# Seven half-size block products for the value tiles of a feed-forward layer, and an earlier value evacuation in latent attention

## The reference, cut to what matters

```python
q = (_rmsnorm(cq, q_norm) @ w_uq).reshape(B, S, H, MLA_QK)
kv = (_rmsnorm(ckv, kv_norm) @ w_ukv).reshape(B, S, H, MLA_NOPE + MLA_V)
k_nope, v = kv[..., :MLA_NOPE], kv[..., MLA_NOPE:]
```

```python
h = _rmsnorm(x, norm_g)
up = h @ w_up
gate, val = up[..., :D_FF], up[..., D_FF:]
gate = conv(gate, conv_w) + conv_b          # width 3 along the tokens
return (jax.nn.silu(gate) * val) @ w_down   # D_FF = 2816
```

## Time and profile before

| | us |
|---|---|
| median of 3 runs | 2328.27 (2326.47 to 2335.23) |
| the profiled execution | 2325.44 |
| its span, first to last instruction | 2323.6 |
| latent attention up to its loop of scores | about 194 to 235 |
| up projection of `ffn0` | 359 to 577 |
| first tile of its down projection | 577 to 592 |

### The profile page before, as it was taken

How to read it: one execution, slowest core, us unless ns; L and a number is a source line. 1 busy time by engine, 2 the same in 40 slices (tenths; PEclk the granted TensorE clock), 3 DMA queues, 4 the chain that set the end, 5 groups by cost and what they waited for, 6 DMA issues and landing times.

```text
span 2323.6 us, 30116 instructions
## 1 busy us (share of the span) xinstructions
PE 2245.7 (97%) x11716; PEld 1073.1 (46%) x11716; DVE 1298.2 (56%) x2620; ACT 1249.5 (54%) x2233; POOL 241.7 (10%) x324
## 2 busy tenths in 40 slices
PE   7999999999999999999999998999999999999998
PEld 3434554444444454444444446654334444654333
DVE  5565856456546556777664594654335744644233
ACT  7544666657657676665675763732225765522213
POOL 0000000000002330000000000021242000011232
PEclk9999999999999999999999999999999999999999
DMA  5230021331223211222123321468974231358997
GB/s 204 90 111 1 1 73 73 109 109 71 105 107 113 78 73 37 92 109 108 63 100 111 109 78 46 158 244 355 416 296 185 109 145 41 134 181 325 418 407 272
DMA packets 70576, 340.36 MB, mean 146 GB/s; under 512 B 13237, under 2 KB 13547, under 8 KB 55565
## 3 DMA queue, kind: packets, MB, share of 16 engines
q1 hardware_dynamic: 49680, 261.38, 29.4%
q0 software_dynamic: 20752, 77.04, 9.3%
HBM read 367.93 MB, written 28.34 MB: 171 GB/s over the span
## 4 chain that ended last, share of the span: by engine, by line
PE 86%; DVE 6%; ACT 3%; DMA 2%; issue 2%; POOL 1%; DVEq 0%; SPq 0%; POOLq 0%; ACTq 0%
PE PB L406 12%; PE PB L401 12%; PE PB L407 12%; PE PB L3417 8%; PE PB L3443 4%; PE PB L1753 3%; PE PB L1757 3%; PE PB L1754 3%; PE PB L470 1%; PE PB L471 1%; PE PB L472 1%; PE PB L3366 1%; DVE WS L321 1%; DMA T<-moe_x,small 1%; PE PB L4068 1%
## 5 line engine op out<-in xcount | busy, mean ns | idle before, releaser
L406 PE MATMUL PB<-AS,WS 128*128 128x512 f16 x1336 | 507.2, 380 | 4.8 <-DVE WS L321 4.8
L407 PE MATMUL PB<-AS,WS 128*128 128x512 f16 x1336 | 507.1, 380 | 0.0
L401 PE MATMUL PB<-AS,WS 128*128 128x512 f16 x1336 | 479.4, 379 | 2.5 <-DVE AS L1221 2.5
L321 DVE SCALAR_TENSOR_TENSOR WS<-raw,sc,WS 128x1024 f16<-128x1024 f32 (+3 forms) x288 | 329.2, 1191 | 89.5 <-ACT WS L308 89.5
L308 ACT ACTIVATE WS<-raw,sc 128x1024 f16<-128x1024 f32 (+3 forms) x288 | 288.5, 1057 | 77.0 <-DVE sc L288 74.9
L262 ACT ACTIVATE junk<-raw 128x1024 f16<-128x1024 f32 (+3 forms) x288 | 280.0, 972 | 7.0
L3417 PE MATMUL PB<-T 128*64 128x512 f32 x736 | 212.4, 595 | 11.9 <-issue 9.1
L406 PEld LDWEIGHTS PB<-AS,WS 128*128 128x128 f16 x1336 | 130.9, 98 | 165.4 <-DVE WS L321 5.5
L401 PEld LDWEIGHTS PB<-AS,WS 128*128 128x128 f16 x1336 | 130.8, 98 | 161.5 <-DVE AS L1221 4.1
L407 PEld LDWEIGHTS PB<-AS,WS 128*128 128x128 f16 x1336 | 130.9, 98 | 158.3 <-issue 4.8
L276 POOL PARTITION_ALL_REDUCE sc<-sc x72 | 31.6, 439 | 1250.9 <-ACT junk L262 1239.1
(11 more groups left out here) (667 smaller groups left out, 3653.0 us busy)
## 6 DMA issues: line engine op xcount, KB each, us to landing
T<-in_moe_up SPq DMA_DIRECT2D x26, 2048.0 KB, 12.7
raw<-in_w_up SPq DMA_DIRECT2D x22, 2048.0 KB, 7.7
T<-in_moe_down SPq DMA_DIRECT2D x26, 1024.0 KB, 14.5
raw<-in_w_down SPq DMA_DIRECT2D x16, 1408.0 KB, 6.0
raw<-in_w_in_even SPq DMA_DIRECT2D x8, 2048.0 KB, 7.8
raw<-in_w_in_odd SPq DMA_DIRECT2D x8, 2048.0 KB, 7.6
WS<-in_moe_up SPq DMA_DIRECT2D x6, 2048.0 KB, 16.2
moe_y<-X SPq DMA_DIRECT2D x18, 512.0 KB, 11.1
```

Source lines behind the costliest of these rows:

```text
L321: e.scalar_tensor_tensor(lo[q], raw[q], s, hi[q], MUL, SUB).then_inc(*k.s("dve_split").up("lo", i, q))
L401: return e.matmul(bank, wh[:, q, c, :], act.lo[c], start=False, stop=c == kt - 1)
L406: e.matmul(bank, wh[:, q, c, :], act.hi[c], start=c == 0, stop=False)
L407: e.matmul(bank, wl[:, q, c, :], act.hi[c], start=False, stop=False)
```

## The change

**In the up projection of `ffn0`**, chunks 3 to 10 (`SEVEN_FROM = 3`) keep their two gate tiles. Their two value tiles are a product of a 256 x 1024 by a 1024 x 512 matrix. It is cut into 2 x 2 blocks on the weight side (two output tiles by two halves of the inputs) and 2 x 2 on the activation side (two halves of the inputs by two halves of the tokens). It is then computed as seven block products instead of eight. Each product is 12 matmuls of 128 x 256 (4 input blocks, 3 parts). Three products use weight blocks as they are, four use sums of blocks, and so it is on the activation side.

- The activation sums are made once, during t = 5 to 9: four DVE sums, four ACT high parts, four DVE low parts, each of 128 x 1024.
- The weight sums are made for each chunk by POOL in fp32 (`pool_seven`: one operation of 128 x 1024 and two of 128 x 512), split by ACT and DVE (`act_seven_hi`, `dve_seven_lo`: parts "1" of 1024, "t" of 2048 and "b" of 512 elements). This happens in the chunk's own time, no longer in that of the chunk before. Only the two gate quarters are still split a chunk ahead.
- The products are put together by one ACT operation (`act_seven`) and five DVE operations (`dve_seven`), and two DVE products with the gate follow. They run behind the chunk, in the next one's time.
- The sum over partitions for the chunk's scale moves from POOL to PE: a matmul with ones of 4 columns behind the gate tiles. It waits for the four squares of the next chunk. So do the two sums for the scales of `hid`; the first stands in chunk 8, the second in the first down tile.
- The high and low parts of hidden tiles 0 to 15 are made in chunks 8, 9 and 10 by the table `SEVEN_EARLY`, at the end of each chunk's list.
- The down projection now waits, before its first matmul, for the last assembly (`up` of chunk 10), since the products lie in banks 4 to 7.
- The normed activation is kept in fp32 in `k.h`, as the sums need it.

**In latent attention**, PE makes queries 3 before it turns queries 0; ACT evacuates values 0 and turned queries 1 before the root for queries 3 and values 1 before the table load; DVE handles queries 2 before turned queries 0.

```diff
@@ even0_pe
     turned("k", 2)
+    queries(3)
     turned("q", 0)
-    queries(3)
     turned("k", 3)
@@ even0_act, query_squares
+        if j == 3:
+            values(0)
+            turned("q", 1, 0)
         w.wait_ge(*v.past("qss", j))
         act_root(e, m.qss[:, 8 * j:8 * j + 8], 96, k.col("eps6"), a, "q", j)
         if j == 3:
+            values(1)
             e.preload_act_table_set(LN_EXP)
@@ even0_dve
-    queries(0)
-    queries(1)
+    for j in range(3):
+        queries(j)
     turned(0)
-    queries(2)
     turned(1)
@@ new
+def pool_seven(k, e, w, n):
...
+    w.wait_ge(*k.s(f"raw{n % 2}").past(n))
+    if is_seven(n - 1):
+        w.wait_ge(*k.s("dve_split").past("lo", n - 1, "t"))
...
+    e.tensor_tensor(t[:, 0:1024].rearrange("p (a b) -> p a b", a=2), raw[:, 3072:4096].rearrange("p (a b) -> p a b", a=2),
+                    by2[:, :, 1024:1536], SUB).then_inc(*g.up("t13", n))
+    w.wait_ge(*g.now())
+    e.tensor_tensor(t[:, 1024:1536], raw[:, 3584:4096], t[:, 0:512], SUB).then_inc(*g.up("t2", n))
+    w.wait_ge(*g.now())
+    e.tensor_tensor(t[:, 1536:2048], raw[:, 1536:2048], t[:, 1024:1536], SUB).then_inc(*g.up("t", n))
@@ new
+def pe_seven(k, e, w, i, act):
...
+    for q in (0, 2):
+        t = 4 * i + q
+        w.wait_ge(*v.past("conv", t // 2 - 2))
+        pe_tile(k, e, w, name, t, act, k.PB[q][:, :], False)
+    w.wait_ge(*k.s("act_junk").past("w", n + 1, 3))
...
+    e.matmul(z.weight, k.cst("ones"), st, start=True, stop=True).then_inc(*p.up("sum", n + 1))
+    if i == EARLY // 2:
+        w.wait_ge(*v.past("sum", "hid", 0))
+        e.matmul(z.total, k.cst("ones"), k.small[:, 288:289], start=True, stop=True).then_inc(*p.up("total", "hid", 0))
...
+        for c in range(4):
+            e.matmul(out, w_hi[c], a_hi[c], start=c == 0, stop=False, skip_group_check=True)
+            e.matmul(out, w_lo[c], a_hi[c], start=False, stop=False, skip_group_check=True)
+            x = e.matmul(out, w_hi[c], a_lo[c], start=False, stop=c == 3, skip_group_check=True)
...
+    product(z.P1, ..., "P1", 1)
+    product(z.P6, ..., "P6", "t")
+    product(z.P2, ..., "P2")
+    product(z.P7, ..., "P7")
+    product(z.P5, ..., "P5")
+    product(z.P4, ..., "P4")
+    product(z.P3, ..., "P3", "b")
@@ new
+def dve_seven(k, e, w, i):
...
+    e.scalar_tensor_tensor(u2, z.P6, sc, p1, MUL, ADD)
+    e.scalar_tensor_tensor(z.up[:, 0, :], z.P2, sc, p1, MUL, ADD)
+    e.scalar_tensor_tensor(u34, two(z.P75), sc, u2.unsqueeze(1).to_broadcast([128, 2, 256]), MUL, ADD)
+    e.scalar_tensor_tensor(z.up[:, 3, :], z.P5, sc, u34[:, 0, :], MUL, ADD)
+    e.scalar_tensor_tensor(z.up[:, 1:3, :], two(z.P43), sc, u34, MUL, ADD)
@@ new
+SEVEN_EARLY = {8: range(0, 4), 9: range(4, 10), 10: range(10, 16)}
@@ ffn_pe
+    if not layer:
+        for i in range(SEVEN_FROM, UPS):
+            pe_seven(k, e, w, i, act)
+
     def free(bank):
+        if not layer:
+            w.wait_ge(*v.past("up", UPS - 1))
@@ ffn_act
+            for part in (1, "t", "b"):
+                act_seven_hi(k, e, w, n, part)
+            act_square(k, e, w, n + 1, 0)
+            act_square(k, e, w, n + 1, 1)
+            act_evac(k, e, w, m.up, 4 * i)
+            conv(2 * i, k.PB[0][:, :])
+            act_square(k, e, w, n + 1, 2)
+            act_square(k, e, w, n + 1, 3)
+            gate(2 * i)
+            if i > SEVEN_FROM:
+                square(2 * i - 2)
+                square(2 * i - 1)
+            act_evac(k, e, w, m.up, 4 * i + 2)
+            conv(2 * i + 1, k.PB[2][:, :])
+            hi_quarter(n + 1, 0)
+            gate(2 * i + 1)
+            hi_quarter(n + 1, 2)
+            act_seven(k, e, w, i)
...
+            for x in SEVEN_EARLY.get(i, ()):
+                hi(x)
@@ ffn_dve
+            if i > SEVEN_FROM:
+                hids(i - 1)
+            for part in (1, "t", "b"):
+                dve_seven_lo(k, e, w, n, part)
+            k.s("dve_split").mark("lo", n, 3)
+            taps(i)
+            conv(2 * i, k.PB[0])
+            if i == EARLY // 2:
+                total(0)
+            dve_seven_scale(k, e, w, n + 1)
+            if i == EARLY // 2:
+                scale(0)
+            conv(2 * i + 1, k.PB[2])
+            for q in ((0, 2) if is_seven(n + 1) else range(4)):
+                dve_lo_quarter(k, e, w, n + 1, q)
+            for x in SEVEN_EARLY.get(i, ()):
+                lo(x)
+        hids(UPS - 1)
+        total(1)
```

More of the change, by code:

```diff
@@ L505, in act_square_sum, with norm_tile @@
     e.activation(k.junk[:, 0:S], a, ACT.Square, accum_out=k.small[:, 256 + i:257 + i]).then_inc(*k.s("act_junk").up(*event))
+def norm_tile(k, stage, tmp, i):
+    return k.h[i] if stage == "ffn0" else tmp[i % 2]
 def dve_norm(k, e, w, stage, name, tmp):
@@ L539, in act_norm @@
         w.wait_ge(*v.past("h", "norm", i))
-        e.activation(k.as_hi[i], tmp[i % 2], ACT.Identity, scale=k.sc[:, 64 + which:65 + which]).then_inc(
+        e.activation(k.as_hi[i], norm_tile(k, stage, tmp, i), ACT.Identity, scale=k.sc[:, 64 + which:65 + which]).then_inc(
             *a.up("hi", "norm", i))
@@ L1159, in even0_act @@
     query_squares(3)
-    values(0)
-    turned("q", 1, 0)
-    values(1)
     values(2)
@@ L1704, in ffn_pool @@
         s5_pool(k, e, w)
+    if layer == 0:
+        pool_ahead(k, e, w, m.up, range(4 * SEVEN_FROM))
+        for i in range(SEVEN_FROM, UPS):
+            pool_seven(k, e, w, FIRST[m.up] + i)
+        pool_sum(k, e, w, place(m.down, 1)[0])
+        pool_ahead(k, e, w, m.down, range(1, 8))
+        return
     for g, tiles in enumerate((range(2 * EARLY), range(2 * EARLY, 2 * FF))):
@@ L1718, in ffn_pe @@
     act = k.normed_parts(m.stage, 2 * layer + 1)
-    for t in range(2 * FF):
+    for t in range(2 * FF if layer else 4 * SEVEN_FROM):
         if t >= 4:
@@ L1750, in pe_down @@
             w.wait_ge(*act.hi_ready(c))
+        if c == EARLY // 2 and (name, t) == ("w_down0", 0):
+            w.wait_ge(*act.sig.past("sum", "hid", 1))
+            e.matmul(seven_at(k).total, k.cst("ones"), k.small[:, 288:289], start=True, stop=True).then_inc(
+                *k.s("pe_ffn0").up("total", "hid", 1))
         if c == EARLY:
@@ L1786, in gate, with conv, square, hi_quarter @@
         e.activation(m.cv[i % 3], m.cv[i % 3], ACT.Silu).then_inc(*a.up("gate", i))
-    for t in range(2 * FF):
+    def conv(i, bank):
+        w.wait_ge(*v.past("taps", i // 2))
+        if i >= 3:
+            w.wait_ge(*v.past("hid", i - 3))
+        e.activation(m.cv[i % 3], bank, ACT.Identity, scale=m.tap[(i // 2) % 2][:, 1, i % 2:i % 2 + 1],
+                     bias=k.col(f"cb{layer}", i)).then_inc(*a.up("conv", i))
+    def square(i):
+        w.wait_ge(*v.past("hid", i))
+        act_square_sum(k, e, w, i, m.hid[i], m.stage, "hid", i)
+    def hi_quarter(n, q):
+        if not is_seven(n) or q % 2 == 0:
+            act_hi_quarter(k, e, w, n, q)
+    for t in range(2 * FF if layer else 4 * SEVEN_FROM):
         i = t // 2
@@ L1853, in scale @@
     def scale(g):
-        w.wait_ge(*k.s(f"pool_{m.stage}").past("total", "hid", g))
+        if layer == 0:
+            w.wait_ge(*k.s("pe_ffn0").past("total", "hid", g))
+            e.tensor_copy(k.small[:, 289:290], seven_at(k).total).then_inc(*v.up("total", "hid", g))
+            w.wait_ge(*v.now())
+        else:
+            w.wait_ge(*k.s(f"pool_{m.stage}").past("total", "hid", g))
         scale_of(e, w, v, k.small[:, 289:290], 20, m.s[g], m.inv[g], k.small[:, 290:291], "inv", "hid", g)
@@ L1859, in lo, with lo_quarter, taps, conv @@
         e.scalar_tensor_tensor(m.lo[i], m.hid[i], m.s[int(i >= EARLY)], m.hi[i], MUL, SUB).then_inc(*v.up("lo", "hid", i))
-    for t in range(2 * FF):
+    def lo_quarter(n, q):
+        if not is_seven(n) or q % 2 == 0:
+            dve_lo_quarter(k, e, w, n, q)
+    def taps(i):
+        n = FIRST[m.up] + i
+        dve_tile_scale(k, e, w, m.up, 4 * i, act)
+        src = k.cols[:, COL[f"cw{layer}"][0]:COL[f"cw{layer}"][0] + 3 * FF].rearrange("p (j t) -> p j t", j=3)
+        w.wait_ge(*k.s("dve_split").past("sc", n))
+        e.tensor_scalar(m.tap[i % 2], src[:, :, 2 * i:2 * i + 2], k.tile_scale(n), None, MUL).then_inc(*v.up("taps", i))
+    def conv(i, b):
+        c, tap = m.cv[i % 3], m.tap[(i // 2) % 2]
+        w.wait_ge(*v.past("taps", i // 2))
+        w.wait_ge(*a.past("conv", i))
+        e.scalar_tensor_tensor(c[:, 1:S], b[:, 0:S - 1], tap[:, 0, i % 2:i % 2 + 1], c[:, 1:S], MUL, ADD).then_inc(
+            *v.up("conv_left", i))
+        w.wait_ge(*v.now())
+        e.scalar_tensor_tensor(c[:, 0:S - 1], b[:, 1:S], tap[:, 2, i % 2:i % 2 + 1], c[:, 0:S - 1], MUL, ADD).then_inc(
+            *v.up("conv", i))
+    def hids(i):
+        z = seven_at(k)
+        dve_seven(k, e, w, i)
+        for j in range(2):
+            x = 2 * i + j
+            w.wait_ge(*v.now())
+            w.wait_ge(*a.past("gate", x))
+            e.tensor_tensor(m.hid[x], z.up[:, 2 * j:2 * j + 2, :].rearrange("p c t -> p (c t)"), m.cv[x % 3], MUL).then_inc(
```

(2 more changed lines are left out.)

168 lines of the change are left out of this document (155 added, 13 removed).

## The result

| | before | after |
|---|---|---|
| median, us | 2330.62 of 4 runs | 2357.77 of 4 runs (2354.56 to 2358.99) |
| ratio of the runs | | 1.0117, 95% interval 1.0097 to 1.0136 |
| span of the profiled execution | 2323.6 | 2356.7 |
| totals of the attention block to totals of `ffn0` | 349.8 | 376.7 |

A forecast was written before the change was run, and what follows sets the result against it. PE was taken to bound the up projection, ACT and DVE latent attention. `ffn0` at +6.4 us and attention at -5.3 gave +1.1 on a median of 2328.3, so 2329.4 us; range 2320 to 2340.

The forecast's parts named there:

- latent attention: Latent attention: reordering removes PE's idle and half clock and brings later scores sooner, 5.3 us saved.
- chunk 3: Up projection, chunk 3: saves only 0.1 us, as squares end at 11.2 because weight parts wait for `hid` 5 and ACT.
- chunks 4 to 7: Steady up chunks: PE stays the bound and each saves 0.95 us, 3.8 in all.
- The saving on PE: Up chunks: 256-column matmuls cost 0.109 us each, so a chunk takes 19.8 against 20.72, saving 0.95 us.
- the last rival: Seven products: a 256-column matmul costs 0.134 us as part of its weight load stays bare; 2341 us, chance 0.05.
- I cost them at nothing: Up chunks: POOL's three weight-sum operations, 5.1 us a chunk, run beside side taps from PSUM and add no time.
- the slack of 0.4: Chunks 4 to 7: the square for PE's matmul with ones ends at 10.0, PE's gate tiles at 10.4.
- the chain over ACT and DVE: Chunks 4 to 7: ACT and DVE work stays behind PE, which remains the bound by 0.4 to 0.7 us.
- The price of the overlap: POOL beside DVE in the up chunks: 1.94 us lost in 4.5 of POOL, giving 2.2 a chunk, used only in a rival.
- The rival built on it: Every chunk: POOL meets low parts, quarters or `hid`; steady chunks lose 1.4 us each, about +10, 2340 us, chance 0.10.
- Half clock behind a wait: Clock falls after idle: 1.7 us lost in the first down tile, 1.7 us regained in latent attention.
- The end: From last product to second down tile: DVE's late low parts and assembly stall PE, 23.0 us against 15.3, 7.7 lost.

The follow-up runs named there:

- the one-input form: Changed kernel with the tile scale reading one SBUF tensor and a scalar operand in up chunks 3 to 10; ratio 1.0048 to the kernel before.
- POOL later: Changed kernel with POOL's first weight sum of a chunk waiting for the taps of the chunk before; ratio 1.0049 to the kernel before.
- partition sum on PE: Changed kernel with tile scale and taps before the low parts, and chunk 3's partition sum moved from POOL to PE; ratio 1.0012 to the kernel before.
- taps first: Changed kernel with tile scale and taps ahead of the three low parts in DVE's list, chunks 3 to 10; ratio 1.0025 to the kernel before.
- early sums: Changed kernel with tile scale and taps before the low parts, and activation sums in t = 3 to 6; ratio 1.0016 to the kernel before.
- the version with everything mended: Changed kernel with taps before low parts, earlier activation sums, chunk 3's partition sum on PE and a new order at the end; 2320.81 us, ratio 0.9971.
- the trace with the products alone: Changed kernel without the reordering in latent attention; ratio 1.0122 to the kernel before.

## Why the prediction was wrong

| term, us | forecast | measured |
|---|---|---|
| latent attention | -5.3 | -4.7 |
| chunk 3 | -0.1 | +8.8 |
| chunks 4 to 7 | -3.8 | +3.6 |
| chunk 8 | +0.9 | +4.7 |
| chunk 9 | -0.1 | +0.9 |
| chunk 10 | +1.8 | +1.5 |
| first down tile | +7.7 | +7.4 |
| `ffn0` in sum | +6.4 | +26.9 |

The measured chunks are distances of their first matmuls less 20.72; the first down tile is the rest of the stretch. Chunks 4 to 9 make 12.2 us of the 20.5 by which `ffn0` was missed, chunk 3 makes 8.9, and chunk 10 and the end give 0.6 back.

- **The saving on PE** was right: 84 matmuls at 0.109, chunks of 19.67 once nothing waits (forecast 19.8), so 1.05 us saved and not 0.95. The fp32 row of the trace was the one to go by, and the 0.134 of the last rival did not come.
- **"I cost them at nothing"** is the step that failed in chunks 4 to 9. The prediction saw that POOL starts when low part "t" is done, and named as its neighbours the side taps from PSUM. Between them stands the tile scale, 0.15 us in the earlier trace rows, and it reads two SBUF tensors. It ended up in the sum as part of "scale and taps, 0.4". 2.18 us more, less the slack of 0.4 that the prediction gave, is 1.8; measured is 1.68. So the chain over ACT and DVE was right to a tenth, and one row in it was held up. The experiments with the one-input form and with POOL later show it: each alone takes 13 to 14 us off the stretch.
- **The price of the overlap** was taken from four long operations (1.94 us lost in 4.5). In these rows the cost goes by what is left of the operation that runs, not by the length of the one that is held up: the tile scale ends with POOL's operation or 0.02 us behind it, whether that makes 0.57 us (chunk 3 with the partition sum on PE), 1.71 (taps first), 2.13 (early sums) or 2.33. That is what the Trainium skill, "SBUF — State Buffer", section "SBUF: two separate sides", says of the lock (whoever starts first has the ports for its whole instruction, the other blocks); the prediction named the rule and did not carry it through DVE's list row by row; the trace agrees, by 2.33 us. The rival built on it, with a chance of 0.10, had the right cause and the wrong rows. It let POOL meet low parts, quarters and `hid`, and none of these carries the loss in a steady chunk. That its 2.2 us a chunk is near the 2.18 measured is luck. It gave 1.4 us a steady chunk where 1.84 came (0.95 forecast gain turned into 0.89 loss), and 2340 in all, far below 2358.
- **Chunk 3** failed for a second reason. The forecast had the squares end at 11.2 us into the chunk, held by `hid` 5 and ACT. They ended at 18.5, since POOL began its weight sums at 408.17 and needed 5.9 us, with ACT idle for them for 3.4. Of the wait of 7.82 the overlap in the tile scale is 1.7 to 2.2 (6.11 and 5.58 are left). The taps' place is another 0.7 to 1.3 (4.86 left). The late start of POOL's work is the rest but 0.66, shown by the version with everything mended. The "issue" of 6.73 ahead of an elementwise row stood in the earlier trace rows; the forecast put no price on it.
- **Half clock behind a wait** was priced at the end and left out in the chunks. Chunk 3 is 27.5 by its wait (20.72 - 1.05 + 7.82) and took 29.5; its first products start 0.213 apart; chunk 8 is 23.1 by its waits and took 25.4, at a granted clock of 0.93. In latent attention it was taken as sure to go with the idle time; the trace with the products alone has that idle and full clock, so 1.7 us of this term hang on the execution.
- **The end** was right, by size and cause. The remedy that it suggests, the assembly ahead of the low parts, took 4.0 us off the wait and brought 0.9: the first down tile needs those high and low parts itself (waits of 0.76 and 0.52), and the second waits for its low quarters (1.34).

What stays open: in the two profiled executions the kernels are 22.2 us apart at the end of `ffn0` (+26.9 - 4.7) and 33 at the end of the span, while the ratio of the times stands for 23 to 32. Nothing is changed behind `ffn0`, and the stretches there spread as widely in the other traces, so no cause is shown for the difference. The granted clock is 0.5 for 31 us behind `ffn0` in the trace after and for 16 in the one before. Were PE busy in all of it, that would be up to 7.6 of the 10.9 us, by an estimate from these two figures.

## What to carry to other kernels

Before work is given to POOL, list every DVE operation that can fall beside it and count its SBUF tensor inputs; a tiny one ahead of a waiting engine cost the remainder of POOL's operation here (2.33 us for 0.15), and the form with a scalar operand (0.20) or another place in the list (0.15) cost next to nothing. An idle time "issue" ahead of a POOL row is a price of its own: see what kind of operation stood before it. When a faster engine leaves the others tenths of a microsecond of slack, one small operation that is held up can cost more than the loop was to gain. A mend at the head or the end of the loop can pay little until the next limit is mended too: 0.3 and 1.1 us alone in chunk 3, and 4.4 for the partition sum on PE once the other edits were in (350.2 to 345.8).
